# Pooling and output-gate columns of a projection moved between the steps of a gated linear attention

## The chip, the cores and the metric

The kernel runs on one core of a Trainium2 chip. The metric is the device time of one launch in microseconds (us); lower is better. Engines are named as the profile names them: PE (TensorE, matmuls), DVE (VectorE), ACT (ScalarE), POOL (GpSimd), SP (SyncE, which issues the DMAs).

## The reference, cut to what matters

A backbone of two layers over 512 latent tokens and 256 context tokens, model width 1024, all in float32. Each layer is FFN, token mixer, FFN. The change is in the token mixer:

```
h      = modulate(rmsnorm(x))                       # (tokens, 1024)
proj   = h @ w_in                                   # k 256, v 512, a 32, q 256, r 512, pool 512, gates 2 x 1024
g_f,g_b= log_sigmoid(a @ w_up + b) / 16             # forget gates, two directions
o      = gla_chunked(q, k, v, g_f) + gla_chunked(flipped, g_b)    # chunks of 64 tokens, 4 heads (dk 64, dv 128)
y_gla  = (rmsnorm(o) * silu(r)) @ w_br_gla
y_pool = (window means of pool columns - themselves) @ pool_w * pool_scale @ w_br_pool
out    = (sigmoid(gate_p) * y_pool + sigmoid(gate_g) * y_gla) @ w_out
```

The scan over chunks, S = S * decay + k^T v, runs in both directions, over the context's four chunks first and then the latent's eight, so it has 11 steps after the first chunk. In the second layer the context needs only its states, so q, r, the pooled columns and the gates are computed for the 512 latent tokens alone.

## The kernel before

Activations are stored transposed, channels on the 128 partitions and the NT = 768 tokens along the free axis. A float32 product is made of three passes of the faster fp32r type: weights and activations are split into hi + lo (`whi`, `wlo`, `hhi`, `hlo`), and `unit_products` adds hi*hi, lo*hi and hi*lo. The work is cut into **units** of 128 output columns: 8 K chunks (DC = 8), for each of which hi*hi and lo*hi, and then 8 K chunks of hi*lo. For every unit SP loads `wraw` (one of 4 slots), ACT makes `whi` (`split_hi`, L1271), and DVE makes `wlo` (`split_lo`, L1441), one unit ahead or so. Two units form a pair, which shares a set of PSUM banks that is freed by `pair_free`. The order of every engine's queue is written out by hand, and semaphores tie the queues together.

The mixer of a layer, as PE's queue has it:

- `proj_tensor`: 17 units in the order k k, a, q q, u u u u (the pool columns), v v v v, r r r r. `PROJ_JOBS` puts small float32 products between pairs: z (`wup`, L513, for the forget gates), vt (L519, transposes of v), and behind the last v unit vt 2 and 3 and four pw products (L523, `poolw` times `u`), of which each waits until ACT and DVE have read the one before from the single PSUM area. POOL computes the window means (`pool_groups`) as the u units come out.
- `gla_tensor`, after all 17 units: head pair 0 and then head pair 1, each with transposes of `kend` (L548), 11 steps of `kv_products` (L569, two PSUM banks in turn, read by DVE's state updates L873 and L875 in four instructions a step), `scores` (L560, masked by DVE in L855 and L856) and outputs per block of 128 tokens (L598, copied by ACT), and last the sums of squares (L609).
- Meanwhile DVE and ACT form h a second time, from the saved `rstd` (L1512, ACT L1341, L1522), for the area that held `hhi` and `hlo` is reused by the attention's tiles `qbd`, `kt`, `kpad` and `states`.
- `gates`: the first pair of gate units goes through `first_pair`, which takes h chunk by chunk, with the transposes of the reciprocal norms (`onorm_tensor`, L629) between the token halves; DVE scales the heads (L901), ACT and DVE split them (L740, L910), and then the two half-length branch units (`yphi`, `yghi`) of the pair follow. Seven more such groups and the `out` phase come after.

What holds up a step is seen in lines such as these two, of `gla_tensor` and of DVE's part:

```
pe.wait_ge(pair_free, p0 + 9)
pe.wait_ge(misc_free, MISC * (l + 1))
...
at_least(pe, kv_used, kv0 + s - 1)
```

Of the kernel before, what the change touches and what calls it, by code (L numbers as in the profile page):

```python
# [21 lines left out]
P = 128  # L22
# [9 lines left out]
DK = 64  # L32
# [54 lines left out]
def make_plan():  # L87
# [24 lines left out]
    for layer in range(DEPTH):  # L112
        for ffn in range(2):
            first = layer == 0 and ffn == 0
            if ffn == 1:
                add("proj", layer, 9, units=17)
# [26 lines left out]
PROJ_JOBS = {2: [("z", 0)], 3: [("z", 1)], 4: [("z", 2)], 5: [("z", 3)],  # L143
             6: [("vt", 0), ("vt", 1)], 7: [("vt", 2), ("vt", 3)] + [("pw", g) for g in range(4)]}
MISC = 12
FWD = [*range(SEQ // CHUNK, NCH), *range(SEQ // CHUNK)]
BWD = [*range(NCH - 1, SEQ // CHUNK - 1, -1), *range(SEQ // CHUNK - 1, -1, -1)]

# [12 lines left out]
def build(nc, t):  # L161
# [24 lines left out]
    rstd = sb("rstd", [P, NT])  # L186
# [55 lines left out]
    lay.skip(48, "pad_proj")  # L242
    kq = lay("kq", [P, 4, NT])
    vt = lay("vt", [P, NBLK, VW])
    rsil = lay("rsil", [P, 4, NT])
    bsum = lay("bsum", [P, 4, NT])
    vf = lay("vf", [P, 2, NT])
# [4 lines left out]
    lay.skip(1, "pad_proj2")  # L252
# [3 lines left out]
    poolw = lay("poolw", [P, 4, P])  # L256
    recs = lay("recs", [P, 4, POOL_REC])
    lay.done()

    lay = Layout()  # L260
    qbd = lay("qbd", [P, 2, 2, NT])
    kt = lay("kt", [P, 2, NT])
    kpad = lay("kpad", [P, 2, NBLK, 2, P])
    states = lay("states", [P, 2, NCH, DV])
    lay.skip(6, "pad_gla")
    lay.skip(48 + 24, "pad_gla2")
    ex = lay("ex", [P, 2, 3, NT])
# [5 lines left out]
    lay.skip(120, "pad_onorm")  # L273
    osq = lay("osq", [P, HEADS, NT])
    lay.done()
# [69 lines left out]
    e_ready = sem("e_ready")  # L345
# [122 lines left out]
    def h_base(a):  # L468


        return 2 * DC * a - DC * max(0, a - (4 * DEPTH - 2)) + DC * max(0, a - (4 * DEPTH - 1))

    def follows_norm(ph):
        return ph["kind"] in ("proj", "gates") or (ph["kind"] == "up" and ph["third"] == 0)
# [6 lines left out]
    def is_split_ahead(ph, i, h, s):  # L481
        return follows_norm(ph) and isinstance(i, int) and i == h == 0 and s == 1

    def peeled(ph, a):

        return (a == 0 and follows_norm(ph)) or (a == 1 and ph is plan[0])

    def proj_tensor(pe, l, u0, p0, unit_products, first_pair, inside):


        unit, misc = u0, MISC * l
        for n, units in enumerate(proj_pairs()):
            pair = p0 + n
            pe.wait_ge(pair_free, pair - 1)
            if n == 0:
                first_pair(unit, pair % 2, BOTH, h_base(4 * l + 1), inside=inside)
                unit += 2
                continue
            for s, (what, _, _, _) in enumerate(units):
# [3 lines left out]
                mm.then_inc(w_used, 1)  # L503
                unit += 1
            for job, g in PROJ_JOBS.get(n, []):

                at_least(pe, misc_free, misc)
                if job == "z":
                    pr, d = g // 2, g % 2
                    pe.wait_ge(pair_free, p0 + 2)  # L510
                    pe.wait_ge(s_mix, 16 * 5 * (l + 1))
                    for t0, c in BOTH:
                        mm = nc.tensor.matmul(ps[:, 3072 + t0:3072 + t0 + c],  # L513
                                              wup[0:2 * RANK, d, pr * P:(pr + 1) * P],
                                              alow[0:2 * RANK, t0:t0 + c], start=True, stop=True)
                elif job == "vt":
                    pe.wait_ge(pair_free, p0 + (6, 7)[g // 2])
                    for b in range(NBLK):
                        mm = nc.tensor.transpose(bank(6, b * P, P), vf[:, g % 2, b * P:(b + 1) * P], ident[:])  # L519
                else:  # L520
                    pe.wait_ge(pooled, 4 * l + g + 1)
                    for t0, c in parts_of("proj", l, "u"):
                        mm = nc.tensor.matmul(ps[:, 3072 + t0:3072 + t0 + c], poolw[:, g, :],  # L523
                                              u[:, g, t0:t0 + c], start=True, stop=True)
                mm.then_inc(misc_ready, 1)
                misc += 1

    def blocks(l):
        return NBLK if l < DEPTH - 1 else XBLK
# [5 lines left out]
    KV_STEPS = NCH - 1  # L535

    def gla_tensor(pe, l, p0):

        pe.wait_ge(pair_free, p0 + 9)
        pe.wait_ge(misc_free, MISC * (l + 1))  # L540

        def transpose_kend(pr, d):

            pe.wait_ge(kend_ready, 4 * l + 2 * pr + d + 1)
            if pr and d:
                pe.wait_ge(kpad_ready, 4 * l + 3)
            for b in range(NBLK):
                mm = nc.tensor.transpose(kend_bank(pr, d, b * P, P), ex[:, d, 2, b * P:(b + 1) * P], ident[:])  # L548
            mm.then_inc(kend_t, 1)

        for d in range(2):
            transpose_kend(0, d)
# [1317 lines left out]
```

## Time and profile before

| what | value |
|---|---|
| time, median of 3 runs | 3251.37 us (3248.11 to 3253.08) |
| the profiled execution: its own time, its span | 3254.89 us, 3253.1 us |
| PE busy | 3105.7 us, 95% |
| PE weight loads (overlap PE) | 2625.9 us, 81% |
| DVE, ACT, POOL busy | 1555.0 (48%), 836.4 (26%), 224.2 us (7%) |
| mean granted TensorE clock | 0.972 of full speed |
| chain of work that ended last | PE 89%, DVE 7%, ACT 2% |
| data moved | 273.42 MB, mean 84 GB/s |

A busy PE is not PE at its peak: a matmul at the lower clock counts as busy for twice as long. The span cut in 40 slices of 81 us shows PE at 9 tenths almost everywhere; it shows 7 at the very start, in the two slices from 813 us and in two from about 2520 us, and the granted clock is lower in the same places. Those are the mixers of the two layers.

### The profile page before, as it was taken

To read this page: it belongs to the slowest core of one execution; us is meant where nothing else is said; L and a number is where in the kernel's file an instruction comes from. 1 tells how busy PE (TensorE), PEld (TensorE's weight loads), DVE (VectorE), ACT (ScalarE), POOL (GpSimd) and SP (SyncE) were. 2 spreads that over 40 slices of the span, in tenths; PEclk is the share of its full clock that TensorE was granted. 3 is DMA by queue.
4 is the path that set the end of the run, shared out by engine and by line. 5 is a ranking of instruction groups with operands and counts; after the bars stand their busy time and mean duration, and the time that the engine had idled before them with its cause. 6 is when DMAs were issued, how large, how long until landed. Compare 5 with 4: busy or idle time off the path is not lost.

```text
span 3253.1 us, 43346 instructions
## 1 busy us (share of the span) xinstructions
PE 3105.7 (95%) x16692; PEld 2625.9 (81%) x16692; DVE 1555.0 (48%) x2699; ACT 836.4 (26%) x1108; POOL 224.2 (7%) x213
## 2 busy tenths in 40 slices
PE   7999999999779999999999999999999779999998
PEld 4888888887568888888888888888887558888886
DVE  2565565544473336565555652222254464443333
ACT  3211111242332223112212311121234233332223
POOL 1000000107000010000000100000015000100001
PEclk9999999999789999999999999999999889999999
DMA  6334334221002214244442332212113103323331
GB/s 199 111 110 123 110 103 137 59 69 49 10 10 62 64 59 123 84 130 136 122 120 82 96 97 59 65 58 65 57 39 85 33 10 94 103 84 91 90 97 65
DMA packets 455603, 273.42 MB, mean 84 GB/s; under 512 B 9754, under 2 KB 453828, under 8 KB 455492
## 3 DMA queue, kind: packets, MB, share of 16 engines
q1 hardware_dynamic: 454404, 268.42, 28.8%
q10 hardware_dynamic: 1088, 3.47, 0.3%
q8 instruction: 75, 1.23, 0.2%
q14 instruction: 36, 0.29, 0.0%
HBM read 269.77 MB, written 2.10 MB: 84 GB/s over the span
## 4 chain that ended last, share of the span: by engine, by line
PE 89%; DVE 7%; ACT 2%; issue 1%; DMA 0%; POOL 0%; ACTq 0%; DVEq 0%; POOLq 0%
PE ps L1030 51%; PE ps L1036 26%; PE ps L1058 2%; PE ps L1178 2%; PE ps L1099 2%; DVE states L875 1%; PE ps L1183 1%; DVE hlo L1522 1%; PE ps L1138 1%; PE ps L598 1%; PE ps L569 1%; DVE htmp L1512 1%; PE ps L560 1%; PE ps L1077 1%; PE ps L523 1%
## 5 line engine op out<-in xcount | busy, mean ns | idle before, releaser
L1030 PE MATMUL ps<-hhi,whi 128*128 128x512 f32 (+1 forms) x3088 | 880.8, 353 | 0.9 <-ACT whi L1271 0.9
L1030 PE MATMUL ps<-hlo,whi 128*128 128x512 f32 (+1 forms) x3088 | 872.9, 350 | 0.0
L1441 DVE TENSOR_TENSOR wlo<-wraw,whi 128x1024 fp32r<-128x1024 f32 x371 | 461.2, 1245 | 663.3 <-ACT whi L1271 659.7
L1271 ACT ACTIVATE whi<-wraw 128x1024 fp32r<-128x1024 f32 x371 | 391.5, 1056 | 1033.7 <-PE ps L1036 999.5
L1036 PE MATMUL ps<-hhi,wlo 128*128 128x512 f32 (+1 forms) x3088 | 615.4, 350 | 6.2 <-DVE wlo L1441 6.2
L1036 PEld LDWEIGHTS ps<-hhi,wlo 128*128 128x128 f32 x3088 | 494.1, 189 | 90.7 <-DVE wlo L1441 6.9
L1030 PEld LDWEIGHTS ps<-hhi,whi 128*128 128x128 f32 x3088 | 495.5, 189 | 87.1 <-issue 2.2
L1030 PEld LDWEIGHTS ps<-hlo,whi 128*128 128x128 f32 x3088 | 495.1, 189 | 83.5 <-issue 0.5
L1456 DVE SCALAR_TENSOR_TENSOR macc<-modraw,cond,macc 128x256 f32<-128x256 f32 x896 | 365.4, 478 | 0.0
L1030 PE MATMUL ps<-mhi,whi 128*128 128x512 f32 (+1 forms) x1184 | 336.1, 351 | 2.6 <-DVE mlo L1657 1.5
L1030 PE MATMUL ps<-mlo,whi 128*128 128x512 f32 (+1 forms) x1184 | 334.2, 349 | 0.0
L1653 DVE TENSOR_TENSOR mtmp<-ps,stmp 128x512 f32<-128x512 f32 (+1 forms) x154 | 82.7, 573 | 384.6 <-ACT stmp L1392 384.6
L1036 PE MATMUL ps<-mhi,wlo 128*128 128x512 f32 (+1 forms) x1184 | 235.9, 349 | 0.0
L1030 PEld LDWEIGHTS ps<-mhi,whi 128*128 128x128 f32 x1184 | 188.8, 188 | 35.8 <-DVE mlo L1657 2.8
L1036 PEld LDWEIGHTS ps<-mhi,wlo 128*128 128x128 f32 x1184 | 188.9, 188 | 32.1
L1030 PEld LDWEIGHTS ps<-mlo,whi 128*128 128x128 f32 x1184 | 188.9, 188 | 31.9
L1392 ACT ACTIVATE stmp<-ps 128x512 f32<-128x512 f32 (+1 forms) x154 | 70.7, 504 | 557.7 <-PE ps L1036 557.6
L1667 DVE SCALAR_TENSOR_TENSOR x<-ps,gate,x 128x512 f32 (+3 forms) x156 | 89.9, 635 | 176.3 <-PE ps L1036 176.3
L1790 POOL MEMSET ssq<- 128x768 f32 x7 | 5.2, 743 | 2448.0 <-PE ps L1036 2050.7
L1657 DVE TENSOR_TENSOR mlo<-mtmp,mhi 128x768 f32 (+3 forms) x88 | 78.5, 892 | 93.3 <-ACT mhi L1396 93.3
L1396 ACT ACTIVATE mhi<-mtmp 128x768 f32 (+3 forms) x88 | 69.8, 793 | 108.4 <-DVE mtmp L1653 108.4
L1058 PE MATMUL ps<-hhi,whi 128*128 128x256 f32 (+1 forms) x240 | 87.1, 363 | 11.0 <-DVE hlo L1522 10.7
(181 smaller groups left out, 2593.7 us busy)
## 6 DMA issues: line engine op xcount, KB each, us to landing
wraw<-in_ffn_up SPq DMA_DIRECT2D x176, 512.0 KB, 3.9
modraw<-in_w_mod SPq DMA_DIRECT2D x66, 1024.0 KB, 5.2
wraw<-in_ffn_down SPq DMA_DIRECT2D x64, 512.0 KB, 3.7
wraw<-in_w_in SPq DMA_DIRECT2D x64, 512.0 KB, 4.0
wraw<-in_ffn_down SPq DMA_DIRECT2D x32, 384.0 KB, 3.1
wraw<-in_w_out SPq DMA_DIRECT2D x16, 512.0 KB, 3.7
first_mod<-in_w_mod SPq DMA_DIRECT2D x6, 1024.0 KB, 12.3
wraw<-in_w_br_pool SPq DMA_DIRECT2D x16, 256.0 KB, 2.7
```

Of the source, the lines that this page charges most:

```text
L1030: nc.tensor.matmul(o, whi[:, slot, k, :], a[:, k * NT + t0:k * NT + t0 + n], start=(k == 0 and a is hi), stop=False)
L1036: mm = nc.tensor.matmul(o, wlo[:, slot, k, :], hi[:, k * NT + t0:k * NT + t0 + n], start=False, stop=k == kk - 1)
L1058: mm = nc.tensor.matmul(o, w[:, (unit + s) % 2, k, :], a[:, k * NT + t0:k * NT + t0 + n], start=(k == 0 and w is whi and a is hhi and open ...
L1099: mm = nc.tensor.matmul(bank(6, 2 * c + h, 1), macc[:, buf, c, h * P:(h + 1) * P], ones[:, 0:1], start=True, stop=True)
L1271: nc.scalar.activation(whi[:, slot2], wraw[:, slot4], ACT.Copy).then_inc(hi_split, 1)
L1392: ins = nc.scalar.activation(stmp[:, h, pt[0]:pt[0] + pt[1]], pair_ps(buf, 0, pt), ACT.Silu)
L1396: nc.scalar.activation(mhi[:, ds((2 * i + h) * NT, c)], mtmp[:, h, 0:c], ACT.Copy).then_inc(mhi_done, 1)
L1441: nc.vector.tensor_tensor(wlo[:, slot2], wraw[:, slot4], whi[:, slot2].bitcast(F32), ALU.subtract).then_inc(lo_split, 1)
L1456: ins = nc.vector.scalar_tensor_tensor(out=macc[:, buf, c, :], in0=modraw[:, buf, k, :], scalar=cond[:, c * DC + k:c * DC + k + 1], in1=ma ...
L1653: ins = nc.vector.tensor_tensor(mtmp[:, h, pt[0]:pt[0] + pt[1]], pair_ps(buf, 1, pt), stmp[:, h, pt[0]:pt[0] + pt[1]], ALU.mult)
L1657: nc.vector.tensor_tensor(mlo[:, ds((2 * i + h) * NT, c)], mtmp[:, h, 0:c], mhi[:, ds((2 * i + h) * NT, c)].bitcast(F32), ALU.subtract).th ...
L1667: ins = nc.vector.scalar_tensor_tensor(out=x[:, ds(n * NT + t0, m)], in0=pair_ps(buf, s, (t0, m)), scalar=gate[:, ds(e * DC + n, 1)], in1= ...
```

## The change

The units of a layer's projection are taken in another order, and the last eight of them are issued in pieces between the pieces of the attention:

- `proj_tensor` now does nine units: k k, a, q q, v v v v. `UNIT_JOBS` puts one z product behind each of units 3 to 6, and vt 0 and 1 behind units 7 and 8.
- `fill_tensor` does the other eight, u u u u and r r r r. `unit_products` gets a callback `between`, called after each K chunk of the hi passes and after every second K chunk of the lo pass: 12 **slots** a unit, 96 in all. `gla_tensor` has become a generator that gives the slot at which its next step is due (`gla_slot`), and that step's instructions are issued there. ACT and DVE have the same schedule in their queues (`fill_to`): the splits and the read-outs of fill units stand between their attention steps.
- The attention's tiles no longer lie over `hhi` and `hlo`, so h is not formed again. `ex` is gone: the exponentials are written straight into `kt` and `qbd` and multiplied in place. `kv_products` uses banks 0 and 1, the outputs one bank (0), `kend` is transposed in halves.
- The four pw products are now in the first gate unit (`gates_steps`, slots 1, 4, 7, 10), in banks 3 and 5 in turn; the transposes of the reciprocal norms are in the second (slots 1 and 9). The gates' first pair starts when the last read-out, the outputs and the roots (`ostd_ready`) are done.
- ACT loads one table set with both Exp and Ln for z. `poolw` is loaded from ACT's queue after the last scores instead of from SP's. POOL clears `kpad` and `qbd` before the window means instead of after them. The copy of `rstd` is gone.

```diff
-    return [two("k", OFF_K, 0), [("a", OFF_AF, 2 * RANK, 0)], two("q", OFF_Q, 0),
-            two("u", OFF_POOL, 0), two("u", OFF_POOL, 1), two("v", OFF_V, 0), two("v", OFF_V, 1),
-            two("r", OFF_R, 0), two("r", OFF_R, 1)]
+    return [two("k", OFF_K, 0), [("a", OFF_AF, 2 * RANK, 0)], two("q", OFF_Q, 0), two("v", OFF_V, 0), two("v", OFF_V, 1)]
+def fill_units():
+    two = lambda what, off: [(what, off + i * P, P, i) for i in range(4)]
+    return two("u", OFF_POOL) + two("r", OFF_R)
...
+def gla_slot(l, kind, pr=0, i=0):
+    lead, chain, out = (5, 1, 1.5) if l < DEPTH - 1 else (8, 1.6, 2)
+    chains = [lead + 4, 0]
+    outs = [chains[0] + chain * KV_STEPS + 1, 0]
+    chains[1] = outs[0] + 2 * out * blocks(l) + 1
+    outs[1] = chains[1] + chain * KV_STEPS + 1
+    if kind == "kend":
+        return lead + i / 2 if pr == 0 else outs[0] + 2 * out * (1 + i / 2) + out / 2
+    if kind == "kv":
+        return chains[pr] + chain * i
+    if kind == "o":
+        return outs[pr] + 2 * out * i
...
+        def between(slot):
+            nonlocal due
+            while due <= slot:
+                due = next(gla, NEVER)
+        for j, (what, _, _, _) in enumerate(fill_units()):
...
+            mm = unit_products(unit, unit % 2, DC, hhi, hlo, outs, None, lambda slot: between(SLOTS * j + slot))
...
+            for s in range(KV_STEPS):
+                yield gla_slot(l, "kv", pr, s)
...
+                kv_products(pr, s)
+                if pr == 0 and s in (1, 2):
+                    transpose_v(pe, l, p0, 1 + s)
+                if s in ((4, 5), (7, 9))[pr]:
...
+                    scores(pr, ((4, 5), (7, 9))[pr].index(s))
...
+        for s in range(KV_STEPS):
+            fill_to(gla_slot(l, "kv", 1, s))
+            state_step(1, s)
+            if s in (1, 2):
+                scale_keys(1, s - 1)
+            if 3 <= s <= 6:
+                scale_queries(1, (s - 3) // 2, (s - 3) % 2)
+            if s == 8:
+                mask_scores(1, 0)
...
+        square_outputs(1)
+        fill_to(NEVER)
+        act.wait_ge(ovar_ready, l + 1)
...
+                            if gates_first:
+                                pe.wait_ge(pair_free, p0)
+                                pe.wait_ge(o_used, o_before(l, 1) + blocks(l))
+                                pe.wait_ge(ostd_ready, l + 1)
```

## Rows read from the trace of the kernel before

**Rows 1.** Layer 0 by stretch: length; PE, PEld, DVE, ACT, POOL busy; clock; DMA share, GB/s

```profile
680.90:804.20 123.30, 120.36 (x655) 101.06 (x654) 49.69 (x44) 40.71 (x48) 63.78 (x85) 0.99 0.29 77
804.20:825.00 20.80, 12.56 (x31) 5.79 (x28) 4.97 (x5) 4.34 (x7) 0.00 (x0) 0.60 0.00 0
...
844.00:945.30 101.30, 70.59 (x344) 57.04 (x344) 64.16 (x135) 28.98 (x48) 13.60 (x8) 0.81 0.01 2
945.30:981.00 35.70, 31.99 (x169) 27.72 (x170) 27.35 (x41) 19.09 (x28) 0.00 (x0) 0.86 0.10 27
```

**Rows 2.** Layer 1 by stretch, the same columns

```profile
2437.90:2541.90 104.00, 97.73 (x461) 77.33 (x461) 49.81 (x42) 39.60 (x44) 45.28 (x47) 0.98 0.34 90
2541.90:2571.80 29.90, 23.10 (x69) 13.78 (x67) 9.11 (x10) 5.84 (x8) 0.52 (x1) 0.71 0.09 24
2571.80:2688.20 116.40, 80.69 (x360) 62.95 (x361) 75.01 (x151) 39.64 (x60) 10.89 (x8) 0.85 0.04 10
```

**Rows 3.** PE in order of time: begins of whole units, and a z product (start, us, group)

```profile
706.54 1.55 PE L513 MATMUL ps<-alow,wup 32*128 32x512 f32 x4
708.02 0.62 PE L1030 MATMUL ps<-hhi,whi 128*128 128x512 f32 x2
...
795.69 0.52 PE L1030 MATMUL ps<-hhi,whi 128*128 128x512 f32 x2
...
804.17 0.82 PE L519 MATMUL ps<-ident,vf 128*128 128x128 f32 x6
...
2446.42 0.40 PE L1030 MATMUL ps<-hhi,whi 128*128 128x512 f32 x1
...
2452.02 0.39 PE L1030 MATMUL ps<-hhi,whi 128*128 128x512 f32 x1
```

**Rows 4.** PE in order of time: steps of the attention in both layers

```profile
873.19 1.13 PE L569 MATMUL ps<-vt,kpad 128*128 128x256 f32 x4 [0.40 <-DVE states L875]
874.72 1.13 PE L569 MATMUL ps<-vt,kpad 128*128 128x256 f32 x4 [0.40 <-DVE states L875]
...
883.61 1.06 PE L598 MATMUL ps<-qbd,states 128*128 128x128 f32 x8
884.50 1.03 PE L560 MATMUL ps<-qbd,kt 128*128 128x256 f32 x4
885.37 0.82 PE L548 MATMUL ps<-ident,ex 128*128 128x128 f32 x6
...
2653.00 3.63 PE L609 MATMUL ps<-ones,osq 128*128 128x1 f32 x32
```

**Rows 5.** Busy time by stretch, inside the first loop of state steps

```profile
871.60:879.30 7.70, 5.65 (x20) 3.39 (x20) 6.93 (x21) 0.00 (x0) 0.00 (x0) 1.00 0.00 0
```

**Rows 6.** DVE groups: masks in the attention, weight splits from 683 to 804 us

```profile
L855 DVE COPY_PREDICATED att<-masks,ps 128x256 f32<-128x256 uint8 x12 | 5.3, 444 | 21.2 <-PE ps L560 21.2
...
L1441 DVE TENSOR_TENSOR wlo<-wraw,whi 128x1024 fp32r<-128x1024 f32 x13 | 17.1, 1331 | 20.8 <-ACT whi L1271 20.8
```

**Rows 7.** DVE in order of time: queries times factors, for head pairs 0 and 1

```profile
851.12 1.91 DVE L837 TENSOR_TENSOR qbd<-kq,ex 64x768 f32<-64x768 f32 x2
...
894.56 5.03 DVE L837 TENSOR_TENSOR qbd<-kq,ex 64x768 f32<-64x768 f32 x2
```

**Rows 8.** POOL in order of time: the scaling of the first two heads

```profile
894.21 4.57 POOL L1814 TENSOR_TENSOR rsil<-bsum,rsil 128x768 f32<-128x768 f32 x2 [44.44 <-ACT bsum L723]
```

**Rows 9.** ACT in order of time: read-outs of r, and the root's table load

```profile
844.03 1.64 ACT L653 ACTIVATE rsil<-ps 128x512 f32<-128x512 f32 x4 [7.36 <-PE ps L1036]
...
949.65 1.28 ACT L736 ACT_TABLE_LOAD   x1
950.94 0.28 ACT L736 ACTIVATE tok<-ps,eps 128x24 f32<-128x24 f32 x1
```

**Rows 10.** PE in order of time: the first branch unit of layer 0 and the next

```profile
969.84 0.98 PE L1030 MATMUL ps<-yphi,whi 128*128 128x512 f32 x2 [3.67 <-ACT whi L1271]
...
976.71 0.52 PE L1030 MATMUL ps<-yghi,whi 128*128 128x512 f32 x2
```

More of the change, by code:

```diff
@@ L115, in make_plan @@
             if ffn == 1:
[L116 removed]
+                add("proj", layer, 6, units=17)
                 add("gates", layer, 2 * DC, parts=parts_of("gates", layer))
@@ L495, in proj_tensor @@
             if n == 0:
-                first_pair(unit, pair % 2, BOTH, h_base(4 * l + 1), inside=inside)
+                first_pair(unit, pair % 2, BOTH, h_base(3 * l + 1), inside=inside)
                 unit += 2
@@ new lines, in fill_tensor @@
+    def fill_tensor(pe, l, u0, p0, unit_products):
+        gla = gla_tensor(pe, l, p0)
+        due = next(gla)
+        def between(slot):
[3 more added lines that the diff above has]
+        for j, (what, _, _, _) in enumerate(fill_units()):
+            unit = u0 + AHEAD + j
+            if j < 2:
+                pe.wait_ge(pair_free, p0 + 4 + j)
+            else:
+                pe.wait_ge(fill_free, (FILL - 1) * l + j - 1)
+            outs = [(pt, fill_ps(j, pt)) for pt in parts_of("proj", l, what)]
+            mm = unit_products(unit, unit % 2, DC, hhi, hlo, outs, None, lambda slot: between(SLOTS * j + slot))
+            mm.then_inc(w_used, 1)
+        between(NEVER - 1)
@@ L616, in onorm_ps @@
+        for h in (2, 3):
+            yield gla_slot(l, "var", 1, h)
+            variances(h)
     def onorm_ps(h, buf):
@@ L676, in gla_scalar, with fill_to, end_factors @@
-    def gla_scalar(act, steps, l, hi_chunk, split_gates):
+                unit += 1
+    def gla_scalar(act, steps, l, u0, p0, split_hi):
         nb = blocks(l)
         c = nb * P
-        def exponentials(pr):
-            if pr:
-                act.wait_ge(prep_ready, 4 * l + 2)
+        fill, done = fill_units(), 0
+        def fill_to(slot):
+            nonlocal done
+            while done < FILL and SLOTS * (done + 1) + 1 <= slot:
+                j = done
+                unit = u0 + AHEAD + j + 2
+                split_hi(unit, unit % 4, unit % 2)
+                what, _, _, idx = fill[j]
+                act.wait_ge(w_used, u0 + AHEAD + j + 1)
+                if what == "r" and idx == 0:
+                    act.wait_ge(kend_t, 8 * (l + 1))
+                for t0, n in parts_of("proj", l, what)[::-1]:
+                    dst = u[:, idx, t0:t0 + n] if what == "u" else bsum[:, idx, t0:t0 + n]
+                    ins = nc.scalar.activation(dst, fill_ps(j, (t0, n)), ACT.Copy if what == "u" else ACT.Silu)
+                ins.then_inc(fill_free if j < FILL - 1 else pair_free, 1)
+                done += 1
+        def end_factors(pr):
@@ new lines, in gla_vector, with gates_ahead_vector @@
+        mask_scores(1, 1)
+        for b in range(2, nb):
+            fill_to(gla_slot(l, "o", 1, b - 1.5))
+            mask_scores(1, b)
+        fill_to(NEVER)
+        dve.wait_ge(ostd_ready, l + 1)
+        v = tok[:].rearrange("p (h b) -> p h b", h=HEADS)[:, :, 0:nb]
+        nc.vector.reciprocal(v, v).then_inc(orec_ready, 1)
+    def gates_ahead_vector(dve, l, buf):
+        c = blocks(l) * P
+        for g in range(4):
+            dve.wait_ge(yp_hi, 4 * l + g + 1)
+            nc.vector.scalar_tensor_tensor(
+                out=yplo[:, g * NT:g * NT + c], in0=ps[:, 512 * pool_ps(g):512 * pool_ps(g) + c],
+                scalar=vecs[:, l, ROW_PS + g:ROW_PS + g + 1], in1=yphi[:, g * NT:g * NT + c].bitcast(F32),
+                op0=ALU.mult, op1=ALU.subtract).then_inc(misc_free, 1)
@@ L1020, in _, with unit_products @@
         def _(pe):
-            def unit_products(unit, slot, kk, hi, lo, outs, chunk_wait):
+            def unit_products(unit, slot, kk, hi, lo, outs, chunk_wait, between=lambda slot: None):
                 pe.wait_ge(hi_split, unit + 1)
```

727 lines of the change are left out of this document (397 added, 330 removed).

## The prediction, made before the changed kernel ran

> **What bounds the kernel now.** I read the page first: PE is busy for 95% of the span and the chain of work that ended last is 89% PE, so time can only be won where PE waits or runs at the lower clock. The slices show two such places, the mixers. There I took busy time by stretch. In layer 0 the stretch of the nine pairs runs at a granted clock of 0.99 with PE hardly waiting; then the pw products take 20.8 us with PE busy for 12.6 at clock 0.60, the attention 101.3 us with PE busy for 70.6 at 0.81, and the first gate pair 35.7 us at 0.86 [rows 1]. Layer 1 has the same picture: 0.98, then 0.71, then 116.4 us at 0.85 [rows 2]. From the second pair of the projection to the end of the first gate group this is 300.1 us (680.9 to 981.0) and 250.3 us (2437.9 to 2688.2).
>
> How much of that is work? I priced every piece at full clock by the distance from begin to begin in PE's timeline. A whole unit takes 8.48 us, a unit of latent tokens alone 5.60, so a slot (a twelfth) 0.706 or 0.467; a z product 1.48; six transposes 0.65 (0.82 with the drain) [rows 3]. A set of scores takes 0.87, and a kv step has the same four records of 256 columns, so 0.87; the eight records of the state products of a block 0.89, so the four with `att` half of it, 0.45; six `kend` transposes 0.65; a sum of squares, 3.63/32, 0.113 a record [rows 4]. A pw product has the width of a z product: 1.48 (about 1.0 for latent tokens).
>
> Layer 0: 17 units 144.2, two half units 8.5, z 5.9, vt 2.6, pw 5.9, kend 2.6, 22 kv 19.1, 12 scores 10.4, 12 output blocks 16.0, squares (48) 5.4, norm transposes 2.6: 223.2 us. Layer 1: 5 whole units 42.4, 12 latent 67.2, half units 5.6, z 5.9, vt 2.6, pw 4.0, kend 2.6, kv 19.1, 8 scores 7.0, 8 blocks 10.7, squares 3.6, norm transposes 1.7: 172.4. So 76.9 and 77.9 us are waiting, low clock and seams: 154.8 us is all that the change can win, and all of this work stays.
>
> **The change, part by part.** *Removed.* The second forming of h is work of DVE and ACT; its price is in the waits above and goes with them. So are the single-buffered pw products and the pause before z's table loads, which PE never saw (clock 0.99 in that stretch). The `rstd` copy lies under PE's products and is worth nothing.
>
> *z twice as dense.* One z now comes each unit instead of each pair, at the same cost to PE. In the nine pairs DVE was busy for 49.7 of 123.3 us and ACT for 40.7 [rows 1]. Six splits of 1.33 fewer leave DVE some 42 us for the seven units, four z and two transposes that now make this stretch, 67 us of PE's (61 in layer 1): busy for six to seven tenths. A unit needs its `wlo` only 8 of 12 slots in, so a backlog of a few us is absorbed. Zero. If that cover failed, a unit would wait about 2 us, twice a layer. SP's queue has one load fewer and each fill unit waits for a split as before, at a slower pace; its loads stay hidden. Zero too. ACT's `poolw` load is issued over 20 slots before its use.
>
> *Seams.* Each piece between K chunks breaks a stream of fp32r products. The trace of before has only the exits: the first product behind z takes 0.46 instead of 0.353 (708.02 to 708.48), and z's four records take 1.48 where the scores' four would make 1.30 scaled to 768 columns [rows 3, 4]; so 0.09 (behind transposes nothing is lost ahead) to 0.29 for a piece. I take 0.2. Outside the chains there are 38 pieces in layer 0 (8 kend, 8 scores, 12 outputs, 4 squares, 4 pw, 2 norm) and 30 in layer 1: 7.6 and 6.0 us, with 3 to 11 and 3 to 9 as bounds.
>
> *The chains of state steps.* This is the step that decides. `gla_slot` gives a kv step each slot in layer 0 and each 1.6 slots in layer 1. PE's own work from the first kv to the first output block, all at full clock, is in layer 0 11 x 0.87 + 12 x 0.706 + vt 1.3 + scores 1.7 = 21.1 us for head pair 0 and 19.8 for pair 1; in layer 1 21.3 and 20.0. DVE can't follow. A state step takes it 1.53 us (873.19 to 874.72, PE waiting 0.40 for it each time) [rows 4], eleven 16.6. In between the new order puts for pair 0 two copies of v (0.96 each, taken as the queries: the same 768 elements), four query products at 0.96, two masks at 0.89 and a split at 1.23 [rows 6, 7], 25.3 us; with 0.95 for the first kv and 1.0 for the places where kv waits behind a set of scores that waits for the queries, 27.3. PE therefore loses 6.2 us in chain 0 of layer 0, seams inside it included. Chain 1 has two keys in place of the copies: 27.3 again, and POOL, which now forms the window means at this time, makes it longer. What POOL costs DVE: two query products took 1.91 us alone and 5.03 beside a POOL product [rows 7, 8], so up to 1.55 each; but 13 splits beside POOL (63.8 us busy of 123.3) took 1.33 instead of 1.23 in the mean [rows 1, 6]. Between 0.1 and 1.55 for each I take 0.4, nearer the case in which POOL runs for long: 3 us for chain 1 of layer 0, 1.6 and 3 in layer 1. With queries of 512 columns (two thirds) and two splits, layer 1's chains are 29.1 and 30.5. Losses: 6.2 + 10.5 in layer 0, 7.8 + 10.5 in layer 1. The state updates I leave at 1.53, with one of their inputs in PSUM; no row shows one beside POOL. If they lost 8% like the splits, a chain would be 1.3 us longer.
>
> The Trainium skill, page "SBUF — State Buffer", section "Who interferes with whom", says that a DVE instruction with two SBUF inputs contends with a GpSimd instruction that reads SBUF, the later one waiting for the whole of the earlier, while one with a single SBUF input does not. The row of 5.03 agrees; the mean of the splits is far milder. By the page each such operation in the chains would stand behind a whole POOL instruction; that is the second case below.
>
> *Start of the fill.* `kend`, its transposes and ACT's eight half copies are ready within a microsecond of slot 9: 1 us a layer.
>
> *A new wait at the end.* The gate pair waits for `ostd_ready`, and ACT comes to the root only after the last unit: split 1.04, two Silu read-outs 0.82, table load 1.28, root 0.28 [rows 9], handovers 0.2: 3.6 us (3.3 in layer 1). Behind a wait of 3.67 PE ran the next half unit in 6.87 us instead of 4.24 [rows 10]: 2.6 more. So 6.2 and 5.9. Behind PE's wait nothing but gate work is queued; DVE's reciprocal and POOL's last scaling follow ACT in the same time.
>
> *In the gate pair.* The norm transposes wait for the fourth pw product's split, 0.5; the first branch unit waits for ACT's last head and split, 1.7 by the same sum of rows instead of 3.67 now; 1.0 for the clock: 3.2 a layer.
>
> Sum: layer 0 223.2 + 7.6 + 16.7 + 1.0 + 6.2 + 3.2 = 257.9 against 300.1, 42.2 less. Layer 1 172.4 + 6.0 + 18.3 + 1.0 + 5.9 + 3.2 = 206.8 against 250.3, 43.5 less. Together 85.7 of the profiled execution's 3254.9 us: 3169.2, or by the same ratio (0.9737) 3166 from the median of 3251.4.
>
> **The rivals.** *DVE held up by POOL.* Each of the some 22 operations with two SBUF inputs in three of the chains costs 1.55 instead of 0.4: 25 us more, 3191. For it: [rows 7, 8], and POOL is busy for 64 us with the means in layer 0, which now lie over both chains. Against: the mild splits of [rows 6]. As said, the skill's page speaks for it.
>
> *Everything meshes.* Seams at 0.09 save 7, no loss to POOL 8, no waits behind scores 4, no clock loss in the gate pairs or after the root 7: 26 less, 3140. For it: in the loop of state steps PE waited 0.40 of every 1.53 us and was still granted the full clock, 1.00 [rows 5].
>
> *The clock falls (slower).* The interleaved stretches hold some 123 + 89 = 212 us of PE work. If waits of a microsecond or two that come again and again keep the clock at 1.2 GHz there, each microsecond of work costs another. From 86 us of work at the low clock, 4 tenths of it, the gain is gone; at half of it the time is 3272, at all of it 3378. For it: the pw products, with waits of 2 us every 5, ran at 0.60 [rows 1]. Against: [rows 5], and in the interleaved order PE is busy for over 8 tenths even in the chains. The Trainium skill, page "TensorE: Matmul & The Clock Gate", section "HAM oscillation — how this bites in real kernels", tells of matmul loops whose waits threw the clock back each time; [rows 5] doesn't agree for short waits.
>
> *The gain isn't there.* An order across queues that I misread makes ACT, DVE and PE wait for each other at each fill unit, 5 us for each of the 16: 3246.
>
> **How the numbers follow.** My forecast has 0.50 with a range of its own of 3148 to 3184; POOL 0.22; all meshes 0.22; clock 0.04; no gain 0.02. Leaving out what lies beyond the first three cases and the outer tails of the second and third gives 3130 to 3202. A change of 0.2%, 6.5 us, is about what a measurement of this kernel can tell from none. Faster 0.94, same 0.02, slower 0.04.
>
> **What would show it.** The same two stretches should take about 258 and 207 us; the pw gap of 20.8 and the attention of 101.3 should be gone, with the fill and attention together near 147 us in layer 0. Waits of PE's kv products for DVE's states should sum to 6 to 10 us a chain and be the largest group of waits in the mixer; PE should wait about 3.6 us for ACT's root before the gates. Query products in the chains should stand between 0.96 and 2.5 us. Wrong would be: a granted clock under 0.9 in the interleaved stretch, kv waits near zero or over 15 us a chain, a PE wait for `wlo` in the z units, or fp32 pieces that take more than 0.3 us over the prices above.

## The result, and the profile after

The changed kernel takes 3163.5 us (median of 4 runs, 3163.3 to 3166.7) against 3251.1 (4 runs, 3248.1 to 3253.1): ratio 0.973, 95% interval 0.972 to 0.974, or 87.6 us less. The forecast was 3166, with 3130 to 3202 as its range. The profiled execution has a span of 3161.9 us instead of 3253.1, the granted clock is 0.986 in the mean instead of 0.972.

From the page of the changed kernel, PE's busy time and the chain that ended last:

```profile
PE 3062.2 (97%) x16692; PEld 2604.5 (82%) x16692; DVE 1515.3 (48%) x2649; ACT 809.0 (26%) x1092; POOL 212.5 (7%) x212
...
PE 90%; DVE 6%; ACT 2%; issue 1%; DMA 0%; POOL 0%; ACTq 0%; DVEq 0%; POOLq 0%
```

PE does the same 16692 matmuls. What changed is the time around them. The mixer of layer 0 by stretch in the changed kernel (columns as in [rows 1]): nine units; chain of head pair 0; its outputs; chain of pair 1; outputs and last fill units; first gate group. Behind them the first four of these stretches of layer 1, without the outputs of head pair 0.

```profile
680.00:749.00 69.00, 69.00 (x376) 56.92 (x375) 35.69 (x39) 25.14 (x33) 5.51 (x4) 1.00 0.34 89
749.00:787.00 38.00, 30.15 (x154) 25.38 (x152) 31.58 (x62) 9.20 (x15) 11.88 (x16) 0.91 0.12 28
787.00:814.00 27.00, 26.02 (x171) 23.35 (x172) 8.14 (x13) 11.82 (x24) 12.28 (x19) 1.00 0.08 21
814.00:849.00 35.00, 26.47 (x109) 21.16 (x108) 27.29 (x56) 6.32 (x10) 28.21 (x43) 0.85 0.12 31
849.00:895.00 46.00, 46.00 (x300) 41.60 (x298) 7.27 (x12) 12.21 (x20) 10.66 (x12) 1.00 0.11 29
895.00:935.60 40.60, 35.21 (x187) 28.93 (x186) 16.80 (x17) 16.25 (x21) 1.99 (x1) 0.96 0.11 27
2390.60:2455.00 64.40, 64.40 (x329) 51.93 (x329) 35.99 (x38) 25.49 (x33) 5.51 (x4) 1.00 0.38 96
2455.00:2495.00 40.00, 30.56 (x130) 24.14 (x129) 32.16 (x63) 9.61 (x16) 14.13 (x17) 0.91 0.16 39
...
2514.00:2543.20 29.20, 22.24 (x93) 16.69 (x91) 24.58 (x54) 7.03 (x10) 18.90 (x24) 1.00 0.10 27
```

The stretch that took 20.8 us at clock 0.60 and the 101.3 at 0.81 of [rows 1] are gone. The whole, from the second pair to the end of the first gate group, is 256.0 us in layer 0 (679.56 to 935.58; before 300.1) and 206.5 in layer 1 (2390.56 to 2597.10; before 250.3): 44.1 and 43.8 less, together 87.9 of the 91.2 us between the two profiled spans. PE is full in the nine units and in the last fill units, nearly full in the output stages, and loses in two kinds of place: the chains of state steps (the rows that begin with 749, 814, 2455 and 2514) and the start of the gates. The waits that make it, PE in order of time:

```profile
755.85 1.13 PE L633 MATMUL ps<-vt,kpad 128*128 128x256 f32 x4 [0.36 <-ACT kpad L831]
...
771.62 2.05 PE L644 MATMUL ps<-qbd,kt 128*128 128x256 f32 x4 [7.05 <-DVE qbd L991]
...
787.05 0.71 PE L664 MATMUL ps<-att,vt 128*128 128x128 f32 x4 [0.49 <-DVE states L1018]
...
820.33 2.08 PE L633 MATMUL ps<-vt,kpad 128*128 128x256 f32 x4 [2.84 <-DVE states L1016]
...
837.82 2.04 PE L644 MATMUL ps<-qbd,kt 128*128 128x256 f32 x4 [3.68 <-DVE qbd L991]
...
899.00 0.98 PE L1204 MATMUL ps<-hhi,whi 128*128 128x512 f32 x2 [3.76 <-ACT tok L875]
```

The largest wait is not one of the kv products (L633) for the states, but one of the scores (L644) for the queries, 7.05 us. DVE at that time:

```profile
763.97 2.67 DVE L991 TENSOR_TENSOR qbd<-kq,qbd 64x768 f32<-64x768 f32 x2
766.67 1.43 DVE L1018 SCALAR_TENSOR_TENSOR states<-states,dec,ps 64x128 f32<-64x128 f32 x4
768.14 3.34 DVE L991 TENSOR_TENSOR qbd<-kq,qbd 64x768 f32<-64x768 f32 x2
771.50 1.30 DVE L1618 TENSOR_TENSOR wlo<-wraw,whi 128x1024 fp32r<-128x1024 f32 x1
...
776.25 1.43 DVE L1018 SCALAR_TENSOR_TENSOR states<-states,dec,ps 64x128 f32<-64x128 f32 x4 [1.98 <-PE ps L633]
```

PE may have two kv products that DVE has not read yet. It issues the fifth while DVE still has queries, a state step and queries to do, and then stands at the scores, which need all of these; fill products behind them in its queue can't pass. Later DVE waits 1.98 us for a kv product that stood behind the scores.

The measure used below, beside the medians: the **mixer time**, from the first transposes of v to the end of the first gate group, both layers together, in the profiled execution. It is 198.4 (737.17 to 935.58) + 154.7 (2442.41 to 2597.10) = 353.1 us in the changed kernel. It leaves out the rest of the program; the begin of layer 0's first v transposes alone lay between 736.97 and 740.37 us in the profiled executions. Each mixer time is of one execution, and the clock behind a wait of 2 to 3 us is not the same in each (see the chains below), which moves it by some 1.5 us for each such wait. "Changed" is the changed kernel; every experiment is an edit of it. Ratios are to the kernel before.

### The profile page after: what moved, and what is told of

Read it like the earlier page. It is cut to its first block, busy times and chain, and to the rows that moved or that the text cites. A ratio compares the mean times of both kernels' runs of the same rounds, so it can differ in the third digit from the quotient of the medians.

```text
span 3161.9 us, 43288 instructions
## 1 busy us (share of the span) xinstructions
PE 3062.2 (97%) x16692; PEld 2604.5 (82%) x16692; DVE 1515.3 (48%) x2649; ACT 809.0 (26%) x1092; POOL 212.5 (7%) x212
## 4 chain that ended last, share of the span: by engine, by line
PE 90%; DVE 6%; ACT 2%; issue 1%; DMA 0%; POOL 0%; ACTq 0%; DVEq 0%; POOLq 0%
PE ps L1204 52%; PE ps L1211 26%; PE ps L1354 2%; PE ps L1275 2%; DVE states L1018 1%; DVE hlo L1699 1%; DVE htmp L1689 1%; PE ps L1359 1%; PE ps L1235 1%; PE ps L1314 1%; PE ps L664 1%; PE ps L644 1%; PE ps L1253 1%; PE ps L633 0%; ACT whi L1448 0%
## 5 line engine op out<-in xcount | busy, mean ns | idle before, releaser
L1204 PE MATMUL ps<-hhi,whi 128*128 128x512 f32 x3136 | 903.5, 355 | 7.2 <-ACT tok L875 7.2
L1204 PE MATMUL ps<-hlo,whi 128*128 128x512 f32 x3136 | 889.1, 351 | 0.0
L1211 PE MATMUL ps<-hhi,wlo 128*128 128x512 f32 x3136 | 632.5, 351 | 0.0
L1204 PEld LDWEIGHTS ps<-hhi,whi 128*128 128x128 f32 x3136 | 504.9, 190 | 91.9 <-issue 11.3
L1204 PEld LDWEIGHTS ps<-hlo,whi 128*128 128x128 f32 x3136 | 503.5, 189 | 85.6 <-issue 0.8
L1211 PEld LDWEIGHTS ps<-hhi,wlo 128*128 128x128 f32 x3136 | 500.8, 188 | 84.4 <-issue 1.0
L1204 PEld LDWEIGHTS ps<-mlo,whi 128*128 128x128 f32 x1184 | 188.8, 188 | 32.2
L1211 PEld LDWEIGHTS ps<-mhi,wlo 128*128 128x128 f32 x1184 | 188.8, 188 | 32.2
L1886 POOL TENSOR_TENSOR ssq<-ssq,sq 128x768 f32<-128x768 f32 (+2 forms) x52 | 84.2, 1619 | 163.3 <-ACT sq L1473 79.2
## 6 DMA issues: line engine op xcount, KB each, us to landing
wraw<-in_w_br_pool SPq DMA_DIRECT2D x16, 256.0 KB, 2.7
```

Source lines behind the costliest of these rows:

```text
L1204: nc.tensor.matmul(o, whi[:, slot, k, :], a[:, k * NT + t0:k * NT + t0 + n], start=(k == 0 and a is hi), stop=False)
L1211: mm = nc.tensor.matmul(o, wlo[:, slot, k, :], hi[:, k * NT + t0:k * NT + t0 + n], start=False, stop=k == kk - 1)
L1886: nc.gpsimd.tensor_tensor(ssq[:, t0:t0 + c], ssq[:, t0:t0 + c], sq[:, j % 2, t0:t0 + c], ALU.add).then_inc(sq_used, 1)
```

## The experiments

The theory to begin with (A): the chains are set by VectorE, whose state steps and the work put between them take 27 to 31 us, and spreading the steps over fill units brings the gain. Rivals: GpSimd, which holds VectorE up, makes most of what is lost (B), the gain comes from the rest of the change (C), TensorE's own seams and clock set the chains (D).

**1. All steps of the attention one behind another.**

```diff
-    lead, chain, out = (5, 1, 1.5) if l < DEPTH - 1 else (8, 1.6, 2)
+    lead, chain, out = (5, 0, 0) if l < DEPTH - 1 else (8, 0, 0)
```

> The spacing of the attention's steps is set to zero, so that all of them follow one another within the second fill unit; order, buffers, the held h and the pw products stay. Theory A (interleaving is what brings the gain: fill units cover the state steps of VectorE): the attention loses again what it lost before, some 45 us of waiting and low clock in layer 0 instead of 23 in the chains, and as much more in layer 1: 3163.5 + 50 = 3213 us (3200 to 3230), and the waits of the kv products for the states stand at 0.4 us for each step again. Rival C (the gain comes from the denser z pairs, the spread pw products and the shorter pause before the gates): under 3185.

Measured: 3194.7 us (ratio 0.983, 0.981 to 0.985), mixer time 376.2, 23.1 more. Spacing is worth 31 us and not 50, and the rest of the change 56. I had put all that the chains lose to the account of the spacing. But without it a chain is shorter as well, the first in layer 0 from 758.00 to 785.73, 27.7 us instead of 31.2: no split stands in it, and the window means, which need a read-out of u, run later, so that DVE works beside no GpSimd (its busy time from 758.00 to 785.70 is 0.00 us).

```profile
758.00 1.99 PE L633 MATMUL ps<-vt,kpad 128*128 128x256 f32 x8 [0.36 <-ACT kpad L831]
...
785.73 0.49 PE L664 MATMUL ps<-att,vt 128*128 128x128 f32 x2 [0.63 <-DVE states L1018]
```

**2. Half the spacing in the chains.**

```diff
+    lead, chain, out = (5, 0.5, 1.5) if l < DEPTH - 1 else (8, 0.8, 2)
```

> A state step each 0.5 slot instead of 1 in layer 0, each 0.8 instead of 1.6 in layer 1. Theory A (VectorE sets the length of the chains): a chain lasts as long as before, but holds 3.9 us (layer 0) or 4.1 us (layer 1) less fill work of TensorE, which comes later instead: 4 chains, 16 us more, 3179 us (3174 to 3185), with these 4 us a chain as more waiting for the states. Rival D (the chains are as long as TensorE's own work with its seams and low clock): within 3 us of 3163.5.

Measured: 3176.6 us (0.977, 0.975 to 0.979), 13.1 more, mixer time 11.6 more. As theory A has it, three quarters or more of its size; D is out: fill work taken out of a chain comes on top.

**3. Wider spacing in the chains.**

```diff
+    lead, chain, out = (5, 1.6, 1.5) if l < DEPTH - 1 else (8, 2.2, 1.5)
```

> A state step each 1.6 slots instead of 1 in layer 0, each 2.2 instead of 1.6 in layer 1 (output blocks of layer 1 each 3 slots instead of 4, so that all ends before the last slot). Theory A: TensorE's own work in a chain rises from 21 to 27 us in layer 0 and from 20 to 24 in layer 1, against some 28 to 31 of VectorE's, so that some 14 us in layer 0 and 6 in layer 1 of waiting and low clock go: 3144 us (3138 to 3152). Rival D: no gain, 3163 within 3 us. Rival E (a long wait of the scores for the queries, with the low clock behind it, makes the loss, wherever it stands): over 3152.

Measured: 3159.5 us (0.972, 0.971 to 0.974), mixer time 4.0 less. A miss for theory A, which had 3138 to 3152: fill work put into the chains is not free either. Its trace shows why: the scores still wait 6.71 us for the queries (773.69), as rival E said. Where PE stands at the scores, the length of its list doesn't matter.

**4. No window means.** GpSimd leaves them out, so u goes into the pw products as it is.

```diff
...
-                    ins = nc.gpsimd.tensor_tensor(tokens, free, tokens, ALU.subtract)
...
+                    ins = nc.gpsimd.tensor_copy(racc[:, 0:GRID_W], src[:, 0:GRID_W])
                     ins.then_inc(pooled, 1)
```

> GpSimd leaves out the window means (it copies one row of 32 elements for each group instead), so that VectorE runs the chains with no other engine at the shared port; u goes into the pw products without its means subtracted. Theory A (contention of half a microsecond for each of some 25 operations with two inputs in SBUF): 12 us less on VectorE, of which 8 show: 3155 us (3150 to 3160), queries at 0.96 us. Rival B (GpSimd holds VectorE up, and that is most of the loss in the chains): 3140 or less. Rival none: 3163.

Measured: 3152.9 us (0.970, 0.968 to 0.971), mixer time 8.0 less, as theory A's sum had it. DVE's groups of layer 0 between 755 and 895 us (operations, busy us, mean ns), first without the means, then changed:

```profile
L1018 DVE SCALAR_TENSOR_TENSOR states<-states,dec,ps 64x128 f32<-64x128 f32 x80 | 27.7, 346 | 7.8 <-PE ps L633 6.3
...
L991 DVE TENSOR_TENSOR qbd<-kq,qbd 64x768 f32<-64x768 f32 x8 | 7.6, 953 | 0.2
```

```profile
L1018 DVE SCALAR_TENSOR_TENSOR states<-states,dec,ps 64x128 f32<-64x128 f32 x80 | 27.7, 347 | 7.1 <-PE ps L633 5.6
L991 DVE TENSOR_TENSOR qbd<-kq,qbd 64x768 f32<-64x768 f32 x8 | 12.0, 1502 | 0.2
```

A query product, with both inputs in SBUF, takes 953 ns alone and 1502 beside GpSimd; a state update, with one input in PSUM, takes 346 and 347. That is the split that the Trainium skill draws ("SBUF — State Buffer", "Who interferes with whom"): by its section only the first kind contends. B's size is not borne out: the whole contention is 8 us (11 by the medians; the profile without the means is of its slowest run). In the changed kernel GpSimd's operations in the second chain of layer 0 took 0.66 us in the mean (28.21 us for 43, the row that begins with 814), and the loss of 0.55 us a product is less than one of them, where the price of 1.55 came from a row beside GpSimd operations of 2.3 us [rows 8]: "behind a whole POOL instruction", as the prediction has it, need not be dear.

**5. The first two scores of a chain later.**

```diff
-                if s in ((4, 5), (7, 9))[pr]:
+                if s in ((7, 8), (8, 9))[pr]:
...
-            if s in (5, 6):
-                mask_scores(0, s - 5)
+            if s in (8, 9):
+                mask_scores(0, s - 8)
...
```

> Of the first two sets of scores of a chain, those of head pair 0 come after state steps 7 and 8 instead of 4 and 5, those of pair 1 after 8 and 9 instead of 7 and 9, each with its masks one step later. Theory F (in TensorE's queue the scores stand in front of kv products and fill, while VectorE still has a step and the queries to do; that wait is the largest part of what the chains lose, and it starves VectorE of kv products for 2 us behind it; at the old spacing, however, VectorE is the bound as soon as it is gone): the waits of 7.05 and 3.68 us in layer 0 shrink under 1 us, the waits for the states grow by most of it, and the time falls by VectorE's idle time alone, 2.0 + 2.5 + 2.4 + 1.1 us with what follows of low clock: 3156 us (3152 to 3160). Rival G (the scores' wait alone is what is lost): all 16.5 us of such waits and some 6 of low clock go, 3141. Rival H (any wait is taken over by the next): 3163.

Measured: 3161.6 us (0.972, 0.971 to 0.973), mixer time 5.5 less. The expected step in the trace is there: no scores wait, and in layer 0 the kv products wait 11.1 us for state updates instead of 1.9. The time is near rival H, since at this spacing the wait only changes its name; the 5.5 us of mixer time are less than the 7.5 that F foretold, and the medians, 2.0 apart, can't tell them from none. About 1.5 of the 5.5 is clock: the wait of 2.84 us at the second chain's start is in both, and behind it the granted clock stayed at 1.00 here (822.46 to 826.46) and was 0.67 in the changed kernel.

**6. Both: wide spacing and later scores.**

> The wide spacing and the later scores together. Theory F: each needs the other; with the scores out of the way TensorE fills the time of VectorE's 28 to 31 us with 24 to 27 us of its own work, and the two gain more than 4 (wide alone) + 7 (order alone) us: 3138 us (3133 to 3145). Rival H: 3152 or more, the sum of the two at best.

Measured: 3149.4 us (0.969, 0.967 to 0.970), mixer time 15.4 less, against 4.0 + 5.5 for the two alone. They do need each other, though the size is 55 to 60% of what I expected, and the time lies outside my range of 3133 to 3145. What is left in the first chain, PE in order of time:

```profile
772.09 1.13 PE L633 MATMUL ps<-vt,kpad 128*128 128x256 f32 x4 [3.08 <-DVE states L1018]
776.39 1.13 PE L633 MATMUL ps<-vt,kpad 128*128 128x256 f32 x4 [1.76 <-DVE states L1018]
...
790.87 0.76 PE L664 MATMUL ps<-att,vt 128*128 128x128 f32 x4 [1.83 <-DVE states L1018]
```

DVE's load is uneven: two queries stand behind each of two steps (3.08 and 1.76 us of waiting), little behind the last ones.

**7. The root before the last fill units.** The rest of the fill stands behind the root on ACT and behind the reciprocal on DVE; for the last unit ACT reads out first and splits then.

```diff
-        fill_to(NEVER)
+        fill_to(gla_slot(l, "var", 1, 3))
         act.wait_ge(ovar_ready, l + 1)
...
+        fill_to(NEVER)
...
+                if j == FILL - 1:
+                    split_hi(unit, unit % 4, unit % 2)
```

> ScalarE takes the root, and VectorE the reciprocal, right after the last sums of squares, ahead of the last fill units' read-outs, and the last read-out goes ahead of the last weight split. The prediction's own step (3.6 + 2.6 us in layer 0, as much in layer 1, for the root behind the last unit): the wait of 3.76 us falls to about 1.0, the low clock behind it goes, 10 us less, 3153 us (3150 to 3157). Rival: the gates' products then wait at the next place (the pw products or the norm transposes), 3160 or more.

Measured: 3157.3 us (0.971, 0.969 to 0.972), 6.2 less, mixer time 8.4 less. PE's wait ahead of the gates is now for the last read-out:

```profile
899.28 0.59 PE L1209 MATMUL ps<-hhi,whi 128*128 128x512 f32 x2 [1.01 <-ACT bsum L802]
```

With the 1.0 and 0.7 us that are left, the root at the end costs 8 us (by the medians) to 10 us (by mixer time) in both layers. At the start of the gates no other wait took its place.

**8. All edits so far**, and ACT splits the weights that are due when the second chain begins ahead of the key factors (`fill_to(gla_slot(l, "kv", 1, 0))` before `key_factors(1)`).

> Wide spacing, later scores, early root, and ScalarE splits the weights due at the start of the second chain ahead of the key factors (VectorE's split there waited 10.47 us and held the first states back, 2.8 us of TensorE's wait). Theory F: 3138 from the first two, 10 less by the root, 2 less by the split: 3126 us (3120 to 3134). Rival H: over 3140.

Measured: 3137.9 us (0.965, 0.964 to 0.966), mixer time 25.6 less, a little more than the parts (15.4 + 8.4), but short of the 3126 expected, by what 6 had fallen short. The last edit removed a wait that the prediction had only as 0.95 us: in the changed kernel DVE's weight split stood in its queue ahead of the second chain's first states and waited 10.47 us for ACT's `whi`, so that PE waited 2.84 us. In number 6 this wait was 2.96 us in layer 1; here there is none, and that chain takes 28.5 us instead of 32.2.

**9. Nothing to cover the attention's start.** Spacing and lead zero, and the work on the end keys of pair 0 comes behind the last v unit and the next weight split, on DVE (cut here: its place in `gla_vector`) and on ACT:

```diff
+    lead, chain, out = (0, 0, 0)
...
-                    if g == 0:
-                        to_end(dve, l, 0)
-                    else:
-                        scale_kend(dve, l, 0)
```

> As the first experiment (all steps of the attention right behind one another), and now they start at slot 0 of the fill, and VectorE forms and scales the keys to their chunk's end for head pair 0 behind the last v columns and the next weight split, instead of beside the last two v units; ScalarE's exponentials of them follow its weight split. Nothing is left that covers the start of the attention. Theory K (of the 56 us that the first experiment kept although its spacing is zero, about half is this start: products of TensorE now run while keys and factors are made): 3194.7 + 2 x 12 = 3219 us (3208 to 3232), with waits of some 5 us of the key transposes and 3 to 4 of the first kv product, as in the kernel before. Rival L (the 56 us lie in the pw products and the gates): within 5 us of 3195.

Measured: 3206.2 us (0.986, 0.984 to 0.987), 11.5 more than 1 by the medians, 18.9 by mixer time (13.2 in layer 0, 5.7 in layer 1; this profile is of its slowest run and that of 1 of its fastest). That is just under my range of 3208 to 3232. In layer 0 the wait of the key transposes that the kernel before had too (5.0 us there) is back:

```profile
PE ps L624 <- DVE kend L965: 6.3, 1, 6.3
```

In layer 1 it is 6.5 us. The wait of the first kv product that I expected too, 3 to 4 us, did not come, and in layer 1 waits of 1.3, 1.2 and 2.4 us that number 1 has there (for `kpad`, `bsum` and `kq`) are absent. So the covered start is worth 11 to 19 us: K in kind and, in layer 0, in size; in layer 1 half.

**10 and 12. The pw products at once; in two banks, and in one as in the kernel before.**

```diff
-        if unit == 0 and slot in (1, 4, 7, 10):
-            pool_products(pe, l, (1, 4, 7, 10).index(slot))
+        if unit == 0 and slot == 1:
+            for g in range(4):
+                pool_products(pe, l, g)
```

Number 12 has these lines besides:

```diff
-        return 3 if g % 2 == 0 else 5
+        return 3
...
-        pe.wait_ge(misc_free, MISC * l + 8 + max(0, g - 1))
+        pe.wait_ge(misc_free, MISC * l + 8 + g)
```

> The four pw products of a layer follow one another at slot 1 of the first gate unit instead of at slots 1, 4, 7 and 10; they keep their two banks. The third has to wait until the first is scaled and split (0.90 + 1.02 us and two handovers, less the second product's 1.1): 1.0 us, the fourth about 1.0, a layer then loses 2 us more and perhaps 1 by the clock: 3168 us (3164 to 3171), of the 12 us a layer that the single bank cost before. Rival: their spreading is the larger part, 3175 or more; or nothing, as two banks are enough, 3163.

> The four pw products follow one another at slot 1 of the first gate unit and share one bank, as in the kernel before: each waits until the one ahead of it is scaled and split. From the rows of before they then begin 4.97 us apart in layer 0 (812.65 to 817.62) and 3.64 apart in layer 1 (2549.35 to 2552.99), so 3 x 4.97 + 1.5 = 16.4 us instead of 5.9, and 3 x 3.64 + 1.0 = 11.9 instead of 4.0: 18 us more than the changed kernel, 3182 us (3176 to 3188), 13 of them beyond the run with two banks (3168.7). Rival: ScalarE's or VectorE's other work in the gates moves with it, and the norm transposes behind it, so that less or more than this sum shows: outside 3176 to 3188.

Measured: 3168.7 us (0.975, 0.973 to 0.976) with two banks, 3184.7 (0.980, 0.978 to 0.982) with one. PE in layer 0, first the kernel before, then one bank, then two banks:

```profile
812.65 2.93 PE L523 MATMUL ps<-u,poolw 128*128 128x512 f32 x4 [2.04 <-DVE yplo L805]
817.62 2.93 PE L523 MATMUL ps<-u,poolw 128*128 128x512 f32 x4 [2.05 <-DVE yplo L805]
```

```profile
908.37 2.36 PE L574 MATMUL ps<-u,poolw 128*128 128x512 f32 x4 [2.13 <-DVE yplo L1072]
912.86 2.90 PE L574 MATMUL ps<-u,poolw 128*128 128x512 f32 x4 [2.13 <-DVE yplo L1072]
```

```profile
906.91 2.82 PE L574 MATMUL ps<-u,poolw 128*128 128x512 f32 x8 [0.84 <-DVE yplo L1072]
```

One bank brings back the waits of 2.1 us for three of the four, and a product of 2.93 us where one at full clock takes half. The two banks are worth 16 us, the spreading 5 (1.2 by mixer time, so near nothing).

**11. One query product a step.** As 8, with the four of head pair 0 behind steps 2, 3, 4 and 5:

```diff
-            if s in (2, 3):
-                scale_queries(0, s - 2, 0)
-                scale_queries(0, s - 2, 1)
+            if 2 <= s <= 5:
+                scale_queries(0, (s - 2) // 2, (s - 2) % 2)
```

> As the version with all edits together (3137.9 us), and VectorE scales the queries of head pair 0 one product a step, at steps 2 to 5, instead of two at steps 2 and 3, where TensorE waited 3.08 and 0.92 us for the states in layer 0 and the output block 1.84. Theory F (with the wide spacing what is left is VectorE's uneven load): 3 us less in layer 0 and 1.5 in layer 1, 3133 us (3130 to 3136). Rival H (VectorE's sum, not its order, sets the chain): 3138.

Measured: 3135.5 us (0.964, 0.963 to 0.965), the fastest version, 28 us under changed. In layer 0 the kv products wait 3.3 us for state updates instead of 6.7. The median is 2.4 us under that of 8, and the intervals overlap. The mixer time is 33.9 less than changed, 8.3 less than 8's, but 8's profile is of its slowest run, 3.2 us above its median. The queries' place is shown in the wait, its worth only as some us.

## Why the prediction was right, and where it was luck

**The stretches.** 257.9 and 206.8 us forecast, 256.0 and 206.5 measured. Of its terms three were off by several us, and in opposite directions.

**Seams: 13.6 us forecast, near nothing measured.** The prices of the pieces already held them. A block of the output stage, PE in order of time:

```profile
852.66 0.61 PE L664 MATMUL ps<-att,vt 128*128 128x128 f32 x4
853.11 1.06 PE L664 MATMUL ps<-qbd,states 128*128 128x128 f32 x8
853.92 1.66 PE L1211 MATMUL ps<-hhi,wlo 128*128 128x512 f32 x8
855.41 1.02 PE L644 MATMUL ps<-qbd,kt 128*128 128x256 f32 x4
856.09 1.05 PE L1211 MATMUL ps<-hhi,wlo 128*128 128x512 f32 x4
856.98 0.49 PE L664 MATMUL ps<-att,vt 128*128 128x128 f32 x3
```

From one output block to the next 4.32 us; the forecast's prices without a seam give 0.89 + 0.45 + 0.87 + 3 x 0.706 = 4.33. In the chain a kv product and a slot take 1.57 (761.97 to 763.54) for 0.87 + 0.706 = 1.58. The right value lies under even my lower bound of 0.09.

**The chains: 35.0 us of loss forecast, 45.7 measured.** From the first kv product to the first output block layer 0 took 31.2 us (755.85 to 787.05) and 34.1 (814.20 to 848.25) for 21.1 and 19.8 of PE's work, layer 1 33.8 (2461.05 to 2494.83) and 28.8 (2514.43 to 2543.22) for 21.3 and 20.0. VectorE sets the chains (experiments 2 and 6), but the step that failed is the waits' place and clock. I wrote that the waits of kv products for states "should sum to 6 to 10 us a chain and be the largest group": they sum to 4.7 us in both chains of layer 0 together, and the largest group is the scores' for the queries, 10.7, which I had entered with 1.0 a chain (16.4 in all four chains, against 4.0). It counts twice: PE stands, and behind each of the two it ran slow. The clock in five stretches of the changed kernel: behind the waits of 7.05 and 2.84 us, among waits of 0.4 to 0.8, behind that of 3.68, and among the four waits of 0.4 to 1.4 us of layer 1's second chain:

```profile
771.60:776.00 4.40, 4.38 (x12) 3.64 (x13) 2.60 (x5) 0.00 (x0) 3.34 (x6) 0.54 0.49 115
...
820.30:825.00 4.70, 4.67 (x16) 3.92 (x17) 4.46 (x10) 0.00 (x0) 4.39 (x5) 0.67 0.45 112
825.00:837.80 12.80, 7.25 (x34) 5.32 (x33) 12.45 (x22) 1.82 (x3) 11.88 (x14) 0.97 0.00 1
837.80:843.00 5.20, 5.18 (x13) 4.27 (x14) 2.63 (x8) 0.00 (x0) 4.49 (x10) 0.50 0.01 3
```

```profile
2514.00:2534.00 20.00, 14.45 (x59) 10.35 (x57) 16.93 (x35) 6.77 (x10) 17.63 (x23) 1.00 0.11 27
```

The lost work is length times one minus clock: 2.0, 1.6 and 2.6 us in layer 0, and 1.7 each behind waits of 1.99 (2468.44) and 3.88 us (2477.97) in layer 1, 9.6 together. I had entered none of it in the chains.

Whether a wait of 1 to 3 us costs clock can't be told from its length. One of 3.08 us at the same place was followed by a granted clock of 1.00 in number 6 (772.09 to 776.39) and 0.66 in number 8 (772.52 to 776.82). And [rows 5], waits of 0.40 us at 1.00, can't be carried to longer ones: in number 1, with no fill work in the second chain of layer 0, waits of 1.3 us that came again and again took the clock down, to 0.65 in the mean from 811 to 825. The same four records took 1.13 and then 2.08 us:

```profile
813.15 1.13 PE L633 MATMUL ps<-vt,kpad 128*128 128x256 f32 x4 [1.30 <-DVE states L1018]
815.58 2.08 PE L633 MATMUL ps<-vt,kpad 128*128 128x256 f32 x4 [1.29 <-DVE states L1018]
817.91 2.08 PE L633 MATMUL ps<-vt,kpad 128*128 128x256 f32 x4 [0.26 <-DVE states L1018]
```

So the rival of the falling clock was not idle. It did not come at its size: from 749 to 895 us and from 2461 to 2543 us the changed kernel is at 0.94, above the 0.9 that I had named as the sign of being wrong, though the second chain of layer 0 alone is at 0.85. My argument against it, PE busy for over 8 tenths even in the chains, was wrong by my own terms: 21.1 of 27.3 us is 0.77, and 19.8 of 30.3 is 0.65. (Eleven state steps of 1.53 us are 16.8, not 16.6; that changes nothing.)

**POOL's price: 0.4 us for each operation, 0.55 measured** (1502 less 953 ns, experiment 4), well inside 0.1 to 1.55; the state updates I rightly left alone. All contention together costs 8 us, so the POOL rival (25 more) was wrong in size. Queries of 768 columns stood between 0.95 and 1.91 us each, against 0.96 to 2.5.

**The root: 6.2 + 5.9 us forecast, about 10 measured** (waits 3.76 and 3.48; the clock behind it 0.63 for 4 us, so 1.5, not 2.6). **The gate pair: 3.2 a layer forecast, 1.6 measured**: only the wait for the split of `whi` (1.62) came; its 1.0 us of clock and the 0.5 at the norm transposes did not. **The start of the fill:** 1.0 forecast, waits of 0.36 and 1.30 us. **z at double density:** PE waited in none of these units, and one took 10.15 us (from one z product to the next, 706.82 to 716.97) for 8.48 + 1.48 = 9.96.

So seams, root and gate pair were priced some 19 us too high and the chains 11 too low. Another 6 us lie in places where I had entered nothing, such as the key transposes of pair 1 that wait for `kpad` (0.9 and 1.2 us) and the clock of 0.67 in the 5.2 us behind the wait at 2494.83 (1.7). The total came out within 3 us because these errors had opposite signs: the mechanism was right, the closeness was luck.

**Where the 88 us come from.** By what each undoing costs: the spacing 31 (1), the two banks and slots of the pw products 21 (12), the covered start 11 to 19 (9). If these add, which no run tested, 16 to 24 us are left to parts that were not undone alone: the order of scores and outputs in the attention, h held on chip, the gates' own start. They stay open.

## What to carry to other kernels

An engine takes its queue in order, so filling a latency-bound chain with other work helps only if no instruction in front of the filler waits for the slow engine's late results: place the consumer behind the last moment at which its input can be ready, then size the spacing to the slow engine's time; each alone gained 4 to 5.5 us of mixer time here, both 15. When pieces are priced from begin to begin in a trace, their entry and exit are in the price, and a seam on top is counted twice. Ask of every transition whether a small, early result (here the root) stands behind late work on its engine only by the order in which it was written.

## What the runs showed of the hardware

The granted clock has two levels here, 1.00 and 0.50 (2.4 and 1.2 GHz). In the mixers of the changed kernel and of numbers 1 to 3 and 5 to 8 every wait of PE of 3.1 us and more was followed by 0.50 to 0.68 in the mean of the next 4.5 us or of the time to the next wait. Between 1 and 3.1 us both came: 1.99 us with 0.57 and 1.84 us with 1.00 in the changed kernel, 2.84 us with 0.67 there and 1.00 in number 5, 3.08 us with 1.00 in number 6 and 0.66 in number 8. Repeated waits of 0.4 to 1.4 us with fill work between them left 1.00 (2514 to 2534), repeated waits of 1.3 us without it 0.65 (number 1). VectorE's state updates with an input in PSUM did not notice GpSimd (346 and 347 ns) where products of two SBUF inputs took 58% longer (953 and 1502). fp32 pieces between fp32r products cost nothing that these begin-to-begin prices did not hold already (4.32 against 4.33 us).
